# V rows gathered in packs of four picks by 32 tokens, and summed by four 32-column products

## The reference

```python
def peer(h, w_query, sub_keys, expert_u, expert_v):
    ...
        qry = (x_blk @ w_query).reshape(T, PEER_HEADS, 2, PEER_DKEY)
        scores = jnp.einsum('thpd,hpnd->thpn', qry, sub_keys).astype(jnp.float32)
        top_s, top_i = lax.top_k(scores, PEER_TOPK)
        ...
        best_s, best_pos = lax.top_k(cand_s, PEER_TOPK)
        idx = jnp.take_along_axis(cand_i, best_pos, axis=-1)
        gate = jax.nn.softmax(best_s, axis=-1)
        u = expert_u[idx]
        act = jax.nn.gelu(jnp.einsum('thkd,td->thk', u, x_blk), approximate=False)
        vsel = expert_v[idx]
        return jnp.einsum('thk,thkd->td', (gate * act).astype(vsel.dtype), vsel)
```

## Time and profile before

| | |
|---|---|
| median of 3 runs | 1902.19 us (1901.16 to 1907.32) |
| span of the profiled execution, first to last instruction | 1833.1 us |
| the profiled execution's own time | not given |
| PE busy | 1408.6 us (77%) |
| DVE busy | 1011.9 us (55%) |
| POOL busy | 1096.8 us (60%) |
| ACT busy | 400.6 us (22%) |
| moved by DMA | 619.35 MB, mean 338 GB/s |
| mean granted clock of PE | 0.898 of full |

### The profile page before, as it was taken

The page is one execution under the profiler, slowest core; times in us unless marked ns, Lnnn a source line. Parts: engine busy times, 40 slices in busy tenths (PEclk is TensorE's granted clock), DMA queues, the critical chain, the costliest instruction groups (busy, mean ns, idle before and its releaser), DMA issues.

```text
span 1833.1 us, 14206 instructions
## 1 busy us (share of the span) xinstructions
PE 1408.6 (77%) x4217; PEld 708.3 (39%) x4217; DVE 1011.9 (55%) x2342; ACT 400.6 (22%) x1019; POOL 1096.8 (60%) x1049
## 2 busy tenths in 40 slices
PE   7988405776887896697868878867899977778886
PEld 6768402222332332245423333323564433223332
DVE  4655697774544444864595456477308355444441
ACT  5645201111211211520112102133213202111111
POOL 2010038777777675776656777557535677777772
PEclk9999757989999898898889898979999988998898
DMA  8250239999999999999988999999978899999995
GB/s 324 80 207 1 84 133 332 389 361 383 409 409 409 366 383 402 409 397 404 404 309 302 409 409 405 401 405 329 397 248 276 318 391 401 389 410 409 409 409 202
DMA packets 182515, 619.35 MB, mean 338 GB/s; under 512 B 18405, under 2 KB 18441, under 8 KB 182441
## 3 DMA queue, kind: packets, MB, share of 16 engines
q0 software_dynamic: 153568, 561.12, 79.5%
q1 hardware_dynamic: 28496, 57.28, 8.3%
q10 hardware_dynamic: 376, 0.05, 0.0%
HBM read 617.34 MB, written 1.05 MB: 337 GB/s over the span
## 4 chain that ended last, share of the span: by engine, by line
PE 30%; DMA 24%; POOL 24%; DVE 11%; issue 9%; ACT 2%; ACTq 0%; DVEq 0%
PE banks L492 19%; POOL arena L308 18%; DMA arena<-in_peer_u_dram,hnT 12%; POOL raw L308 6%; DMA arena<-in_peer_v_dram,hnT 6%; DMA raw<-in_peer_u_dram,hnT 5%; PE banks L370 3%; PE banks L376 3%; DVE arena L1309 2%; PE banks L630 1%; DVE arena L1353 1%; DVE arena L1351 1%; PE banks L516 1%; DVE raw L1309 1%; DMA arena<-in_diff_w_in_dram 1%
## 5 line engine op out<-in xcount | busy, mean ns | idle before, releaser
L492 PE MATMUL banks<-arena,hnT 128*128 128x512 f32 x2048 | 1024.7, 650 | 324.9 <-ACT hnT L851 267.8
L492 PEld LDWEIGHTS banks<-arena,hnT 128*128 128x128 f32 x2048 | 408.5, 207 | 887.5 <-issue 562.7
L308 POOL DMA_INDIRECT arena<-in_peer_v_dram,hnT x512 | 535.6, 1046 | 250.4 <-PE banks L492 143.0
L1309 DVE CUSTOM_DVE_ANT_0 raw<-raw,hrows 128x1024 f32<-128x1024 f32 x256 | 312.4, 1224 | 313.6 <-DMA raw<-in_peer_u_dram,hnT 312.6
L1309 DVE CUSTOM_DVE_ANT_0 arena<-arena,hrows 128x1024 f32<-128x1024 f32 x256 | 311.7, 1224 | 274.6 <-DMA arena<-in_peer_u_dram,hnT 274.2
L308 POOL DMA_INDIRECT raw<-in_peer_u_dram,hnT x256 | 273.1, 1067 | 255.2 <-DVE hnT L1409 140.6
L308 POOL DMA_INDIRECT arena<-in_peer_u_dram,hnT x256 | 274.3, 1071 | 110.0 <-issue 70.4
L851 ACT ACTIVATE hnT<-ident,hnT 128x128 f32<-128x128 f32 x512 | 169.7, 391 | 159.2 <-PE banks L492 119.0
L845 ACT ACTIVATE hnT<-hnT 128x8 f32<-128x8 f32 x64 | 13.4, 209 | 810.8 <-DVE hnT L1309 810.7
L516 PE MATMUL banks<-arena,work 128*128 128x512 f32 x256 | 124.3, 621 | 12.5 <-ACT work L873 6.8
L1041 DVE TENSOR_TENSOR split<-arena,split 128x512 fp32r<-128x512 f32 x96 | 63.5, 689 | 47.6 <-ACT split L716 47.2
(11 more groups left out here) (194 smaller groups left out, 708.9 us busy)
## 6 DMA issues: line engine op xcount, KB each, us to landing
arena<-in_diff_w_in_dram SPq DMA_DIRECT2D x24, 1024.0 KB, 18.1
arena<-in_peer_w_query_dram SPq DMA_DIRECT2D x16, 1024.0 KB, 13.4
arena<-in_gla_w_in_dram POOLq DMA_DIRECT2D x5, 2048.0 KB, 23.0
arena<-in_peer_w_query_dram POOLq DMA_DIRECT2D x4, 2048.0 KB, 16.6
arena<-in_peer_v_dram,hnT POOLq DMA_INDIRECT x512, 7.8
arena<-in_diff_w_out_dram SPq DMA_DIRECT2D x8, 1024.0 KB, 19.7
arena<-in_gla_w_out_dram POOLq DMA_DIRECT2D x2, 2048.0 KB, 10.9
raw<-in_peer_u_dram,hnT POOLq DMA_INDIRECT x256, 7.9
```

The lines of the kernel that those rows point to most:

```text
L308: pool.indirect_dma_start(rows(n), None, table.rearrange("l e d -> (l e) d"), bass.IndirectOffsetOnAxis(ap=places[:, o:o + 1].bitcast(u32) ...
L492: last = nc.tensor.matmul(bank(2 * (tile % NT) + half), diags[:, n % BUFS * P:(n % BUFS + 1) * P], v_rows(n)[:, half * 512:(half + 1) * 51 ...
L1309: V.tensor_tensor_reduce(out=u_rows(n), in0=u_rows(n), in1=hrows[:, o // SLOTS, :], scale=1.0, scalar=0.0, op0=ALU.mult, op1=ALU.add, accu ...
```

## The change

The v rows of four picks are gathered in another arrangement. A pack is four picks x 128 tokens. Before, gather j of a pack held pick j of all 128 tokens. Now gather s holds all four picks of the 32 tokens 32 s to 32 s + 31: partition 32 j + q has the row of pick j of token 32 s + q. The number and the size of the gathers stay.

The weights are laid out in the same way, so the diagonal of a gather is 128 x 32, a stack of four 32x32 diagonals. One product with it contracts over the four picks and gives 32 tokens, in 32 partitions of the PSUM bank. A pack is 2 halves x 4 products, each with its own 32 columns of the array and 32 partitions of the bank (`expert_sums`).

To bring the numbers into the new arrangement ACT copies 32x32 blocks: once a tile the places (`pack_list`) and the gates (`pack_gates`), 16 instructions each, and for each group of eight picks the gelu itself is written in the new arrangement, 16 instructions on 32 partitions x 2 elements. The copies of tile 2 and 3 stand in ACT's order 7 ticks behind the exponentials of their gates, those of tile 0 right behind them, those of tile 1 at tick 80. The v gathers wait for `v_listed` at a tile's first pick, `weigh` for `gates_packed`. `v_used` counts packs, so v buffers and diagonal buffers come free by fours, and PE begins a pack only when `PACK` picks are due and all four are loaded. `PLAN`, the order of the rest, and the u rows are as before.

```diff
+PACK = 4
+LIST = SLOTS
+PACK_T = P // PACK
...
             for t in range(TICKS):
                 for n in range(v_at(t), v_at(t + 1)):
+                    if n % LIST == 0:
+                        pool.wait_ge(S("v_listed"), n // LIST + 1)
                     if n >= BUFS:
-                        pool.wait_ge(S("v_used"), n - BUFS + 1)
-                    gather(peer_v, n, v_rows, "v_loaded")
+                        pool.wait_ge(S("v_used"), (n - BUFS) // PACK + 1)
+                    gather(peer_v, n, v_places, v_rows, "v_loaded")
...
-            def expert_sum(n):
+            def expert_sums(first):
...
-                pe.wait_ge(S("diag_ready"), n + 1)
-                pe.wait_ge(S(f"v_loaded{n % BUFS}"), 16 * (n // BUFS + 1))
+                pe.wait_ge(S("diag_ready"), first + PACK)
+                for n in range(first, first + PACK):
+                    pe.wait_ge(S(f"v_loaded{n % BUFS}"), 16 * (n // BUFS + 1))
                 for half in range(2):
-                    last = nc.tensor.matmul(bank(2 * (tile % NT) + half),
-                                            diags[:, n % BUFS * P:(n % BUFS + 1) * P],
-                                            v_rows(n)[:, half * 512:(half + 1) * 512],
-                                            start=(n % SLOTS == 0), stop=(n % SLOTS == SLOTS - 1))
+                    for j in range(PACK):
+                        n, r0 = first + j, j * PACK_T
+                        last = nc.tensor.matmul(bank(2 * (tile % NT) + half)[r0:r0 + PACK_T, :],
+                                                diags[:, n % BUFS * PACK_T:(n % BUFS + 1) * PACK_T],
+                                                v_rows(n)[:, half * 512:(half + 1) * 512],
+                                                start=(first % SLOTS == 0), stop=(first % SLOTS == SLOTS - PACK))
                 last.then_inc(S("v_used"), 1)
...
-                while summed < v_at(int(t) - SUM_LAG):
-                    expert_sum(summed)
-                    summed += 1
+                while summed + PACK <= v_at(int(t) - SUM_LAG):
+                    expert_sums(summed)
+                    summed += PACK
...
+            def packed(dst, src, function):
+
+                for s in range(PACK):
+                    to = dst[s * PACK_T:(s + 1) * PACK_T].rearrange("p (g j) -> p g j", j=PACK)
+                    for j in range(PACK):
+                        of = src[j * PACK_T:(j + 1) * PACK_T].rearrange("p (g s) -> p g s", s=PACK)
+                        last = A(to[:, :, j], of[:, :, s], function)
+                return last
+
+            def pack_list(n):
+                o = slice(n * LIST % PICKS, n * LIST % PICKS + LIST)
+                act.wait_ge(S("listed"), n + 1)
+                packed(v_places[:, o].bitcast(i32), places[:, o].bitcast(i32), ACT.Copy).then_inc(S("v_listed"), 1)
+
+            def pack_gates(n):
+                o = slice(n * LIST % PICKS, n * LIST % PICKS + LIST)
+                act.wait_ge(S("gates_ready"), n + 1)
+                packed(gates[:, o], ar(A_GG + n * LIST % PICKS, LIST), ACT.Copy).then_inc(S("gates_packed"), 1)
...
-                A(acts[:, o], dots[:, o], ACT.Gelu).then_inc(S("gelu_done"), 1)
+                packed(acts[:, o], dots[:, o], ACT.Gelu).then_inc(S("gelu_done"), 1)
...
-                    act.wait_ge(S("v_used"), n - BUFS + 1)
-                A(diags[:, n % BUFS * P:(n % BUFS + 1) * P], ident[:], ACT.Copy,
+                    act.wait_ge(S("v_used"), (n - BUFS) // PACK + 1)
+                A(diags[:, n % BUFS * PACK_T:(n % BUFS + 1) * PACK_T], ident4[:], ACT.Copy,
...
                 at(GATES[NT + m])
                 gate_exps(NT + m)
+                at(GATES[NT + m] + 7)
+                pack_list(NT + m)
+                pack_gates(NT + m)
...
-                V.tensor_tensor(weights[:, o:o + GRP], acts[:, o:o + GRP], ar(A_GG + o, GRP), ALU.mult
+                dve.wait_ge(S("gates_packed"), g * GRP // LIST + 1)
+                V.tensor_tensor(weights[:, o:o + GRP], acts[:, o:o + GRP], gates[:, o:o + GRP], ALU.mult
```

More of the change, by code:

```diff
@@ L124, in trunk_kernel @@
         iota = sb("iota", [P, TOPK])
+        ident4 = sb("ident4", [P, PACK_T])
         causalT = sb("causalT", [P, P])
@@ L176, in trunk_kernel @@
         words = hnT[:].rearrange("p k t -> p (k t)")
-        dots, acts, weights, places, diags = (words[:, o:o + n] for o, n in (
-            (0, PICKS), (PICKS, PICKS), (2 * PICKS, PICKS), (3 * PICKS, PICKS), (4 * PICKS, BUFS * P)))
+        dots, acts, weights, places, v_places, gates, diags = (words[:, o:o + n] for o, n in (
+            (0, PICKS), (PICKS, PICKS), (2 * PICKS, PICKS), (3 * PICKS, PICKS), (4 * PICKS, PICKS),
+            (5 * PICKS, PICKS), (6 * PICKS, BUFS * PACK_T)))
         def x1(unit, off=0, n=D):
@@ L304, in _, with gather @@
                                    ).then_inc(S("keys_loaded"), 16)
-            def gather(table, n, rows, loaded):
+            def gather(table, n, of, rows, loaded):
                 o = n % PICKS
@@ L309, in gather @@
                     rows(n), None, table.rearrange("l e d -> (l e) d"),
-                    bass.IndirectOffsetOnAxis(ap=places[:, o:o + 1].bitcast(u32), axis=0)
+                    bass.IndirectOffsetOnAxis(ap=of[:, o:o + 1].bitcast(u32), axis=0)
                     ).then_inc(S(f"{loaded}{n % BUFS}"), 16)
@@ L837, in gate_exps, with stacked_identity @@
                 act.preload_act_table(ACT.Gelu)
+            def stacked_identity():
+                act.wait_ge(S("ident_ready"), 1)
+                for j in range(PACK):
+                    r = slice(j * PACK_T, (j + 1) * PACK_T)
+                    last = A(ident4[r, :], ident[r, r], ACT.Copy)
+                last.then_inc(S("ident4_ready"), 1)
+            def packed(dst, src, function):
+                for s in range(PACK):
+                    to = dst[s * PACK_T:(s + 1) * PACK_T].rearrange("p (g j) -> p g j", j=PACK)
+                    for j in range(PACK):
+                        of = src[j * PACK_T:(j + 1) * PACK_T].rearrange("p (g s) -> p g s", s=PACK)
[9 more added lines that the diff above has]
+                packed(gates[:, o], ar(A_GG + n * LIST % PICKS, LIST), ACT.Copy).then_inc(S("gates_packed"), 1)
             ticks = acted = diagonals = 0
@@ L959, in _ @@
             gate_exps(0)
+            stacked_identity()
+            act.wait_ge(S("ident4_ready"), 1)
+            pack_list(0)
+            pack_gates(0)
             at(GATES[1])
             gate_exps(1)
+            at(80)
+            pack_list(1)
+            pack_gates(1)
             at(84)
@@ L1419, in softmax @@
                 ordered()
-                step(V.tensor_tensor(g3, g3, ar(sm + PH, PH).unsqueeze(2).broadcast_to([P, PH, TOPK]), ALU.mult))
-                ordered()
+                V.tensor_tensor(g3, g3, ar(sm + PH, PH).unsqueeze(2).broadcast_to([P, PH, TOPK]), ALU.mult
+                                ).then_inc(S("gates_ready"), 1)
             def add_experts(tile):
                 m = tile % NT
-                dve.wait_ge(S("v_used"), (tile + 1) * SLOTS)
+                dve.wait_ge(S("v_used"), (tile + 1) * SLOTS // PACK)
                 for half in range(2):
```

10 lines of the change are left out of this document (5 added, 5 removed).

## The result

| | median | runs | ratio to before, 95% interval |
|---|---|---|---|
| before | 1901.68 us | 4 (1899.78 to 1907.32) | |
| changed | 1961.31 us | 4 (1955.65 to 1963.45) | 1.0303 (1.0275 to 1.0331) |

The change makes the kernel slower by 3%. The forecast of 1866 us and its range are both missed, on the wrong side. The profiled execution took 1955.65 us, its span is 1953.9.

The account below looks back on a forecast made before the run. The prediction took DMA transfers at about 409 GB/s as the floor, with PE late in some stretches. Terms -20 - 11 - 7 - 3 + 4 + 1 = -36 took 1902 to 1866 us, range 1842 to 1898.

Parts of the forecast that it names:

- Part 3: Mixed u and v gathers: v buffers freed by fours stall POOL 2.5 us once; plus 1 us taken.
- second rival: Ring of two packs starves DMA, stall not absorbed: 1890 us, chance 0.14; sign: POOL waits 2 us per group in 420:580.
- bound of 48: Upper bound for the stall in mixed u and v stretches: 2.5 us x 19 groups.
- V alone: Stretches of v gathers only: two packs alternate, about 10.4 us per eight rows, 1.30 a row, 1.5 at low clock.
- Part 1: Sums on PE: four 32-column products side by side, 1.72 us for four picks, 0.43 a pick.
- (a): 1313 to 1380, query products of tile 3 with 24 v gathers: 47 instead of 67 us, minus 20.
- (b): From `listed` of tile 3 to its first u: 22.2 us replaced by a wait of 11, minus 11.
- (c): The tail, where the last tile's add waits 27.35 us for PE: minus 7 us.
- (d): 596:620, where PE is busy without a break and DMA moves 355 GB/s: minus 3 us.
- Part 2: ScalarE: gelu in 16 instructions, 1.9 us; ACT +50 us, hidden except at waits; tile 2's first u plus 4.
- third rival: Gain goes into new waits, idle PE's clock falls to 1.2 GHz, query and attention products stretch: 1896 to 1904; chance 0.09.

Follow-up runs that it names:

- second profile: The kernel before, code unchanged, profiled again in a single run: 1917.76 us, span 1916.0.
- each gather alone: The changed kernel with each 128x32 gather waited for, summed and freed by itself, v and diagonal buffers freed one by one: 1916.86 us, ratio 1.0052.
- the run with half the columns: The changed kernel with each product on 256 of its 512 columns: 1920.50 us, ratio 1.0061.
- the filled kernel: The changed kernel with four further products with zeros behind each pack but a tile's last, after `v_used`: 1975.42 us, ratio 1.0373.
- the 4/12 kernel: The changed kernel with its 16 buffers split as 4 for u and 12 for v: 1926.81 us, ratio 1.0102.

## Why the prediction was wrong

**What bounded the kernel.** "The chip's transfers are the floor there" rested on an execution that ran its mixed stretches at 409 GB/s. The second profile of the same kernel has 364 there, with POOL issuing for 95 of 100 us. The cover that was to absorb stalls was a queue of transfers ahead of DMA and time to spare on POOL. It did not absorb them: the waits before tile 1's first u are 15.9 us more than before, and their stretch is 16.7 us longer. Whether POOL or a slower DMA sets the pace there stays open. And "about 69 more, which lies outside the span" was false; it changed nothing in the sign.

**Part 3 is the step that failed.** The mechanism stood in it: v row 8g-4 needs the pack that follows group g's gelu, 14.0 us after the issue of u row 8g+7, and POOL gets there in 11.5. Measured: 15.08 (556.32 to 571.40) against 12.23 (to 568.55), a stall of 2.85 where 2.5 was worked out. What was wrong is "once": it was argued that the queue then gets shorter and landing falls by as much. It comes with every group, eight times between 437 and 640 us in tile 0's stretch, 2.3 to 5.8 us each, and is not made good. This is the sign that the prediction itself had named for its second rival. Plus 1 was taken for it. Freed singly, the change costs 2.5 points less, 48 us of 1905 (each gather alone against the changed kernel). That this equals the bound of 48 named beside the term is chance, for the run removes more than part 3's stall: in the two traces, whose spans differ by 36 us, some 23 lie between the first u of tile 0 and that of tile 1, and 20 between `listed` and the first u of tiles 2 and 3 (3.5 and 16.9 us instead of 17.0 and 23.0); other stretches give some back.

**V alone.** 1.30 us a row, 1.5 at the low clock, was forecast; it is 7.00 a pack (1517.40 to 1524.40), 1.75 a row, against 1.72 before. The sum was also wrong in itself: its terms, 4 x 1.24 + 4.5 + 1.7, make 11.2 us and not 10.4, 1.40 a row. The cycle of two packs was the right one, but from short terms. In neighbouring rounds, from the first of four issues to the last is 3.72, from the last issue to the start of the pack 6.25 (1514.21 to 1520.46) where 4.5 was taken, the pack 3.64 where 1.7 was, and 0.30 to the next gather: 13.9 us for eight rows.

**Part 1** was right: four products side by side, 1.92 us a pack where 1.72 was taken. The weight loads lie inside it, four in 0.23 us of each 0.85 (1514.29 to 1515.14, at the low clock), as the witness of the earlier trace rows had it:

```profile
1514.29 0.23 PEld L502 LDWEIGHTS banks<-arena,hnT 128*32 128x32 f32 x4 [0.63 <-issue]
```

The Trainium skill (TensorE: Matmul & The Clock Gate, Part 3) gives 2.38x for three column tiles, from which the prediction worked out 0.54 us a pick as an estimate; the trace has 0.48.

**(a) to (d).** Against the second profile of before: (a) the query products of tile 3 up to its search went from 76.9 us (1358.1 to 1435.0) to 62.1 (1395.9 to 1458.0), minus 15 of the 20. (b) `listed` to first u went from 22.2 to 23.0 us: none of the 11. Thirteen v rows still stood before it, at 1.75 each. (c) the last wait went from 26.31 to 23.10, minus 3 of 7. (d) can't be told from the stalls around it. So (a) and (c) gave some 18 us where PE has work to do, and they lie under a loss elsewhere. Even of (a)'s 15 only 4 are left from the add of tile 1 to the first u of tile 3, for the stretch ahead of the query products, most of it before the attention, is 8 us longer and the search 3. The loss by stretches: from the first u of tile 0 to `listed` of tile 1 plus 3, on to the first u of tile 1 plus 17, on to `listed` of tile 2 plus 12, to its first u plus 12, and from the add of tile 2 to the last v gather plus 15. The stretch behind tile 2's first u, up to the add of tile 1, gives 12 back. With the 4 and the 3 of (c) taken off, this is the 38 us between the two spans, to within 2.

**Part 2** mis-sized a term. The gelu takes 3.44 us, the upper bound, not 1.9; diagonals come 0.23 apart (1.17 for five), not 0.15; the 16 copies take 4.28, not 1.9, since they come 0.27 apart and not 0.11. ACT in all is 189 us busier (400.6 to 589.3), not 50. For tile 2, first u was forecast about 9 us after `listed`, and came after 17.0 (1037.54 to 1054.53): two copy runs of 4.3 in place of 1.9, a pack at the low clock, which freed a buffer at 1050.8, then three v gathers where two were forecast. Only the gelu was found to cost by itself, half a per cent.

**The clock.** The third rival named it ("its clock falls to the 1.2 GHz level while it idles") with 0.09, and gave 1896 to 1904, for the query and attention stretches. In the query stretch the clock held (0.91 at 1405:1461). In the attention of the second tile it fell as that rival had it, first changed, then the second profile of before (columns as in the earlier trace rows):

```profile
1290.00:1350.00 60.00, 26.52 (x117) 13.30 (x115) 47.72 (x113) 33.73 (x113) 35.20 (x32) 0.61 0.93 346
1257.00:1317.00 60.00, 39.91 (x121) 18.02 (x122) 49.53 (x118) 26.00 (x78) 37.79 (x32) 0.77 0.99 383
```

Of the eight groups of 64x256 products, seven had taken 0.70 to 0.81 us and one 1.23; now five take 1.22 or 1.23. Yet from the first to the last product the attention took no longer: 51.2 us (1292.13 to 1343.32) for 52.5 (1255.10 to 1307.61). And the clock fell under the first pack of each group. Part 3 had that pack at 3.4 in its chain, so the low clock was not overlooked there, and the run with half the columns shows that the pack's length counts. How much of the loss a quick clock would save isn't shown, since the filled kernel left those packs slow. The forecast priced the rivals one at a time; but both together, 48 and at most 38 us over 1866, would be 1952, still under the 1961 measured.

## What to carry to other kernels

Before an engine is made faster by handing work on in larger units, follow one buffer all the way round at the new unit: issue, landing, every step before it in its group, the unit's own time at the clock that it will be granted, release. If that is longer than the ring gives, the stall recurs each round, unless the engine that stalls has measured time to spare. The remedy was to keep the narrow products but wait and free by one: neighbouring gathers still ran side by side where they had piled up, and with two buffers moved from u to v, and later lists, the kernel was 0.6% faster than before.

## What was not expected of the hardware

- A gather's issue on POOL is not constant. The mean for v is 1046 ns in the quicker execution of before and 1108 in an ordinary one; single ones go from 0.93 us to 3.06 (in the 4/12 kernel). That difference goes with 409 and 364 GB/s in the mixed stretches of the same program. Why one execution is quicker stays open.
- ScalarE's instructions on 32 partitions come 0.215 us apart for two elements and 0.27 for 32, where eight of 128x128 come 0.30 apart: a small instruction saves little.
- PE's clock follows what PE did before. In the changed kernel the 26 packs that stand by themselves behind a pause of 10 us or more took 3.21 to 3.64 us, and one right behind other products 1.92 (548.45); behind shorter pauses both occur. Products put behind a pack left the first pack after the next pause at 3.2 to 3.6.
